# A float32 transformer kernel on one core: the first blocks of the FFN and of the MLPs get an order of their own, and two helpers move behind them

## The reference

```python
# model 1, behind the attention: D_FF = 2816
h = rms_norm(x, norm2_g)
x = x + (silu(h @ w_gate) * (h @ w_up)) @ w_down

# model 2, in each of two layers: MLP_HIDDEN = 4096
u = rmsnorm(x, norm_mlp[l])
x = x + jnp.square(jax.nn.relu(u @ w_mlp_up[l])) @ w_mlp_down[l]

def rmsnorm(x, g):
    return x * lax.rsqrt(jnp.mean(x * x, axis=-1, keepdims=True) + EPS) * g
```

## Time and profile before

| | us |
|---|---|
| median of 3 runs | 1058.37 |
| lowest and highest | 1055.93 and 1059.07 |
| the profiled execution, its device time | 1054.6 |
| its span, from the first to the last instruction | 1052.8 |
| PE busy in the span | 1030.9 (98%) |
| DVE busy | 708.2 (67%) |
| ACT busy | 535.8 (51%) |
| mean granted clock of TensorE | 0.992 |

### The profile page before, as it was taken

One profiled execution on the slowest core, in us unless ns is written; L12 is line 12 of the kernel. 1 busy time (PEld: TensorE's weight loads), 2 busy tenths in 40 slices (PEclk: granted clock), 3 DMA queues, 4 the chain that ended last, 5 costly groups with the idle time before them and its releaser, 6 DMA issues.

```text
span 1052.8 us, 16387 instructions
## 1 busy us (share of the span) xinstructions
PE 1030.9 (98%) x6205; PEld 896.1 (85%) x6205; DVE 708.2 (67%) x1073; ACT 535.8 (51%) x687; POOL 69.7 (7%) x80
## 2 busy tenths in 40 slices
PE   8999999999999999999999999999999999999997
PEld 6865778888888899998788888888999988888886
DVE  6886766666667686768766656667776777655655
ACT  6546565444457535555635444475354646544443
POOL 1000000000000309000000000011270000000000
PEclk8999999999999999999999999999999999999999
DMA  9964326555556653258365563665632665566521
GB/s 293 246 225 145 120 89 232 200 174 195 174 185 195 200 166 121 81 176 297 128 219 181 189 210 106 225 203 166 192 101 80 230 230 180 179 201 199 165 94 40
DMA packets 130652, 185.12 MB, mean 176 GB/s; under 512 B 4361, under 2 KB 106399, under 8 KB 130591
## 3 DMA queue, kind: packets, MB, share of 16 engines
q1 hardware_dynamic: 130503, 184.25, 54.0%
q10 hardware_dynamic: 88, 0.04, 0.0%
HBM read 180.91 MB, written 1.56 MB: 173 GB/s over the span
## 4 chain that ended last, share of the span: by engine, by line
PE 90%; SPq 2%; ACT 2%; DMA 2%; DVE 2%; issue 1%; ACTq 0%; DVEq 0%
PE wide L559 18%; PE wide L566 9%; PE acc L522 9%; PE acc L523 9%; PE acc L524 9%; PE wide L522 7%; PE wide L523 7%; PE wide L524 7%; PE wide L542 3%; PE wide L535 3%; PE wide L536 3%; DMA raw<-in_w_in 1%; PE acc L702 1%; ACT whi L976 1%; SPq L436 1%; PE acc L736 1%
## 5 line engine op out<-in xcount | busy, mean ns | idle before, releaser
L1270 DVE TENSOR_TENSOR wlo<-raw,whi 128x2048 fp32r<-128x2048 f32 (+1 forms) x178 | 386.8, 2180 | 155.6 <-ACT whi L976 154.5
L976 ACT ACTIVATE whi<-raw 128x2048 fp32r<-128x2048 f32 (+1 forms) x178 | 321.9, 1819 | 106.1 <-PE wide L524 43.9
L559 PE MATMUL wide<-uhl,whi 128*128 128x512 f32 x864 | 208.2, 392 | 0.0
L559 PEld LDWEIGHTS wide<-uhl,whi 128*128 128x128 f32 x864 | 160.9, 188 | 33.9 <-DVE uhl L1295 1.2
L522 PE MATMUL acc<-whi,mhi 128*128 128x512 f32 x376 | 147.9, 393 | 3.0 <-DVE wlo L1270 2.7
L522 PE MATMUL wide<-uhl,whi 128*128 128x256 f32 x512 | 147.5, 288 | 0.8 <-DVE wlo L1355 0.8
L523 PE MATMUL acc<-wlo,mhi 128*128 128x512 f32 x376 | 146.8, 390 | 0.0
L524 PE MATMUL acc<-whi,mlo 128*128 128x512 f32 x376 | 146.4, 389 | 0.0
L523 PE MATMUL wide<-uhl,whi 128*128 128x256 f32 x512 | 145.5, 284 | 0.0
L524 PE MATMUL wide<-uhl,wlo 128*128 128x256 f32 x512 | 145.5, 284 | 0.0
L566 PEld LDWEIGHTS wide<-uhl,wlo 128*128 128x128 f32 x864 | 111.7, 193 | 4.4
(11 more groups left out here) (248 smaller groups left out, 1212.1 us busy)
## 6 DMA issues: line engine op xcount, KB each, us to landing
raw<-in_w_in SPq DMA_DIRECT2D x49, 1024.0 KB, 5.3
raw<-in_w_mlp_up SPq DMA_DIRECT2D x32, 1024.0 KB, 5.5
raw<-in_w_mlp_down SPq DMA_DIRECT2D x32, 1024.0 KB, 4.9
raw<-in_w_gate SPq DMA_DIRECT2D x11, 1024.0 KB, 5.4
raw<-in_w_up SPq DMA_DIRECT2D x11, 1024.0 KB, 5.5
raw<-in_w_down SPq DMA_DIRECT2D x11, 1024.0 KB, 5.5
raw<-in_w_mix_out SPq DMA_DIRECT2D x8, 1024.0 KB, 6.6
raw<-in_w_out SPq DMA_DIRECT2D x4, 1024.0 KB, 9.6
```

Source lines behind the costliest of these rows:

```text
L559: pe.matmul(col[2 * n + c][:], whi_v(u)[:, f, c * P:c * P + P], uhl[:, f, :], start=f == 0, stop=False)
L976: act.activation(whi[:, u.buf, 0:size], raw[:, u.slot, 0:size], ACT.Copy).then_inc(w_hi, 1)
L1270: dve.tensor_tensor(wlo[:, u.buf, 0:size], raw[:, u.slot, 0:size], whi[:, u.buf, 0:size].bitcast(F32), ALU.subtract).then_inc(w_lo, 1)
```

## The change

In the FFN, PE's `spread_rn` moves from the middle of the first up unit (unit 15) to behind the whole of it, and its wait for rb_sb moves from ahead of the first loop block to the first down unit. Two new semaphores, ff_a and ff_d, tell PE that the banks of a gate or an up unit have been read; ff_g and ff_ok no longer let PE go on. On ACT and DVE the first blocks (0, 1 and 2) are written out ahead of the loop: the splits of units 17 and 18 come between the parts of block 0, the copy of rnb comes behind both bank reads, and the scaling by rnb behind the sums. The loops run from the second turn on.

In the MLP, the split of the first down unit (L_MLP + 2) moves ahead of the first block's `low_half` on ACT and ahead of its `ff_split` on DVE. The sum of squares on ACT moves behind block(0), and DVE's two small steps on rn behind block(1). The three blocks that were written out behind ACT's and DVE's loop stand ahead of it now.

The diff, cut to its core:

```diff
@@ -315,6 +315,8 @@
+        ff_a = sem("ff_a")
+        ff_d = sem("ff_d")
@@ -840,16 +842,18 @@
             wide_features_after(1, a_unit(A_FF), 0)
-            wide_features(a_unit(A_FF + 1), 1, lambda: spread_rn(acc[3], 2))
-            pe.wait_ge(rb_sb, 2)
+            wide_features(a_unit(A_FF + 1), 1)
+            spread_rn(acc[3], 2)
             def ff_block(q, turns, start):
                 gate, up, down = (a_unit(A_FF + 2 + 3 * q + r, turns) for r in range(3))
-                pe.wait_ge(ff_g, 2 * turns + q + 1)
+                pe.wait_ge(ff_a, 2 * turns + q + 1)
                 wide_features(gate, 0)
-                pe.wait_ge(ff_ok, 2 * turns + q + 1)
+                pe.wait_ge(ff_d, 2 * turns + q + 1)
                 wide_features(up, 1)
+                if start:
+                    pe.wait_ge(rb_sb, 2)
                 pe.wait_ge(w_lo, down.upto())
                 pe.wait_ge(ff_lo, 2 * turns + q + 1)
                 rows(down, mid(mhi, q), mid(mlo, q), start, False)
@@ -1134,17 +1138,19 @@
             split(a_unit(A_FF + 2))
             squares(1)
             deviations(1)
-            spread_rn(acc[3], 2)
-            def ff_gate(q, count, gate):
+            def gate_low(q, gate):
                 act.wait_ge(used, gate.upto())
                 act.activation(ff_e[q].rearrange("p (c t) -> p c t", c=2), wide[0][:, :, T:2 * T], ACT.Copy).then_inc(ff_b, 1)
+            def gate_sigmoid(q, count):
                 act.wait_ge(ff_g, count)
                 act.activation(ff_h[q], ff_e[q], ACT.Sigmoid).then_inc(ff_act, 1)
-            def ff_up(q, up):
+            def up_low(q, up):
                 act.wait_ge(used, up.upto())
                 act.activation(ff_e[1 - q].rearrange("p (c t) -> p c t", c=2), wide[1][:, :, T:2 * T], ACT.Copy).then_inc(ff_c, 1)
@@ -1153,19 +1159,34 @@
                 act.wait_ge(ff_ok, count)
                 act.activation(mid(mhi, s), h.rearrange("p (c t) -> p c t", c=2), ACT.Copy).then_inc(ff_hi, 1)
-            ff_gate(0, 1, a_unit(A_FF))
-            ff_up(0, a_unit(A_FF + 1))
+            def ff_block(q, turns):
+                j, b = A_FF + 2 + 3 * q, (1 + q) % 2
+                gate_low(b, a_unit(j, turns))
+                gate_sigmoid(b, 2 * turns + q + 2)
+                split(a_unit(j + 3, turns))
+                up_low(b, a_unit(j + 1, turns))
+                ff_split(ff_h[b], b, 2 * turns + q + 2)
+            def ff_weights(q, turns):
+                split(a_unit(A_FF + 3 + 3 * q, turns))
+                split(a_unit(A_FF + 4 + 3 * q, turns))
+            gate_low(0, a_unit(A_FF))
+            split(a_unit(A_FF + 3))
+            up_low(0, a_unit(A_FF + 1))
+            spread_rn(acc[3], 2)
+            gate_sigmoid(0, 1)
+            split(a_unit(A_FF + 4))
             ff_split(ff_h[0], 0, 1)
-            with act.Fori(0, LOOPS) as i:
+            ff_block(0, 0)
+            ff_weights(1, 0)
+            ff_block(1, 0)
+            with act.Fori(1, LOOPS) as i:
                 for q in range(2):
-                    j = A_FF + 2 + 3 * q
-                    b = (1 + q) % 2
-                    split(a_unit(j + 1, i))
-                    split(a_unit(j + 2, i))
-                    ff_gate(b, 2 * i + q + 2, a_unit(j, i))
-                    split(a_unit(j + 3, i))
-                    ff_up(b, a_unit(j + 1, i))
-                    ff_split(ff_h[b], b, 2 * i + q + 2)
+                    ff_weights(q, i)
+                    ff_block(q, i)
@@ -1236,22 +1257,25 @@
                     act.activation(mlp_h[s].rearrange("p (c t) -> p c t", c=2), wide[n][:, :, T:2 * T], ACT.Copy).then_inc(ff_act, 1)
                 split(l_unit(l, L_MLP + 1))
-                squares(3 + 2 * l)
+                split(l_unit(l, L_MLP + 2))
                 low_half(0, 0, l_unit(l, L_MLP))
                 ff_split(mlp_h[0], 0, done + 1)
                 def block(q, turns, count):
                     s = (1 + q) % 3
-                    split(l_unit(l, L_MLP + 2 + 2 * (q % 3), turns))
+                    if q:
+                        split(l_unit(l, L_MLP + 2 + 2 * (q % 3), turns))
                     split(l_unit(l, L_MLP + 3 + 2 * (q % 3), turns))
                     low_half(s, (1 + q) % 2, l_unit(l, L_MLP + 1 + 2 * (q % 3), turns))
                     ff_split(mlp_h[s], s, count)
+                block(0, 0, done + 2)
+                squares(3 + 2 * l)
+                block(1, 0, done + 3)
+                block(2, 0, done + 4)
                 with act.Fori(0, 2) as i:
                     for q in range(6):
-                        block(q, 2 * i + q // 3, done + 6 * i + q + 2)
-                for q in range(3):
-                    block(q, 4, done + 12 + q + 2)
+                        block(3 + q, 2 * i + 1 + q // 3, done + 6 * i + q + 5)
@@ -1516,44 +1540,73 @@
             split(a_unit(A_FF + 1))
             split(a_unit(A_FF + 2))
             inverse(2)
-            dve.wait_ge(rb_sb, 2)
-            def scale_gate(q, count):
+            def gate_sum(q, count):
                 e = ff_e[q].rearrange("p (c t) -> p c t", c=2)
                 dve.wait_ge(ff_b, count)
-                link(dve.tensor_tensor(e, wide[0][:, :, 0:T], e, ALU.add))
+                dve.tensor_tensor(e, wide[0][:, :, 0:T], e, ALU.add).then_inc(ff_a, 1)
+            def gate_scale(q, count):
+                e = ff_e[q].rearrange("p (c t) -> p c t", c=2)
+                dve.wait_ge(ff_a, count)
                 dve.tensor_tensor(e, e, rnb[:].unsqueeze(1).broadcast_to([P, 2, T]), ALU.mult).then_inc(ff_g, 1)
-            def swiglu(q, count):
-                e, h = ff_e[q], ff_h[q]
+            def up_sum(q, count):
                 v = ff_e[1 - q].rearrange("p (c t) -> p c t", c=2)
+                dve.wait_ge(ff_c, count)
+                dve.tensor_tensor(v, wide[1][:, :, 0:T], v, ALU.add).then_inc(ff_d, 1)
+                dve.wait_ge(ff_d, count)
+            def swish(q, count):
                 dve.wait_ge(ff_act, count)
-                dve.tensor_tensor(h, h, e, ALU.mult)
-                dve.wait_ge(ff_c, count)
-                link(dve.tensor_tensor(v, wide[1][:, :, 0:T], v, ALU.add))
-                dve.tensor_tensor(h, h, ff_e[1 - q], ALU.mult).then_inc(ff_ok, 1)
+                return dve.tensor_tensor(ff_h[q], ff_h[q], ff_e[q], ALU.mult)
+            def gated_up(q):
+                dve.tensor_tensor(ff_h[q], ff_h[q], ff_e[1 - q], ALU.mult).then_inc(ff_ok, 1)
             def ff_split(h, s, count):
                 dve.wait_ge(ff_hi, count)
                 dve.tensor_tensor(mid(mlo, s), h.rearrange("p (c t) -> p c t", c=2), mid(mhi, s).bitcast(F32),
                                   ALU.subtract).then_inc(ff_lo, 1)
-            scale_gate(0, 1)
-            swiglu(0, 1)
+            def ff_block(q, turns):
+                j, b, count = A_FF + 2 + 3 * q, (1 + q) % 2, 2 * turns + q + 2
+                gate_sum(b, count)
+                gate_scale(b, count)
+                split(a_unit(j + 3, turns))
+                swish(b, count)
+                up_sum(b, count)
+                gated_up(b)
+                ff_split(ff_h[b], b, count)
+            def ff_weights(q, turns):
+                split(a_unit(A_FF + 3 + 3 * q, turns))
+                split(a_unit(A_FF + 4 + 3 * q, turns))
+            gate_sum(0, 1)
+            split(a_unit(A_FF + 3))
+            up_sum(0, 1)
+            dve.wait_ge(rb_sb, 2)
+            gate_scale(0, 1)
+            link(swish(0, 1))
+            gated_up(0)
+            split(a_unit(A_FF + 4))
             ff_split(ff_h[0], 0, 1)
-            with chain.loop(LOOPS, 4) as i:
+            ff_block(0, 0)
+            ff_weights(1, 0)
+            ff_block(1, 0)
+            with chain.loop(LOOPS - 1, 0) as i:
                 for q in range(2):
-                    j = A_FF + 2 + 3 * q
-                    b = (1 + q) % 2
-                    split(a_unit(j + 1, i))
-                    split(a_unit(j + 2, i))
-                    scale_gate(b, 2 * i + q + 2)
-                    split(a_unit(j + 3, i))
-                    swiglu(b, 2 * i + q + 2)
-                    ff_split(ff_h[b], b, 2 * i + q + 2)
+                    ff_weights(q, i + 1)
+                    ff_block(q, i + 1)
@@ -1663,24 +1716,27 @@
                 done = FF_BLOCKS + MLP_BLOCKS * l
                 split(l_unit(l, L_MLP + 1))
+                square(0, 0, done + 1)
+                split(l_unit(l, L_MLP + 2))
+                ff_split(mlp_h[0], 0, done + 1)
+                def block(q, turns, count):
+                    s = (1 + q) % 3
+                    if q:
+                        split(l_unit(l, L_MLP + 2 + 2 * (q % 3), turns))
+                    split(l_unit(l, L_MLP + 3 + 2 * (q % 3), turns))
+                    square(s, (1 + q) % 2, count)
+                    ff_split(mlp_h[s], s, count)
+                block(0, 0, done + 2)
+                block(1, 0, done + 3)
```

(13 more changed lines are left out.)

## The result

| | before | after |
|---|---|---|
| median of 8 runs, us | 1057.55 | 1050.62 |
| lowest and highest | 1052.47 and 1060.66 | 1045.39 and 1053.83 |
| ratio after to before, 95% interval | | 0.9931 (0.9910 to 0.9951) |
| span of the profiled execution | 1052.8 | 1049.0 |
| mean granted clock | 0.992 | 0.993 |

The account below looks back on a forecast made before the run. PE, busy 98% of the span, was taken as the bound. The FFN's 3.99 us and the MLPs' 3.26 us sum to 7.25 us, so 1058.37 - 7.25 = 1051.1 us, range 1047.0 to 1055.5.

Parts of the forecast that it names:

- The FFN's term: FFN start, unit 15 to unit 16: 10.03 us would become 6.04, a gain of 3.99 us.
- the stall and the clock: Two parts of the FFN gain: 2.19 us of PE's stall before the spread and 1.80 us of lower clock behind it.
- The margins in the FFN: Time in hand before PE needs the gate's banks, 1.2 us, the up's banks, 2.7, and the first down unit, 2.0.
- The MLP's term: PE's wait for wlo before each MLP's first down unit goes: 1.63 us per layer, 3.26 us for both.
- The thin margin: MLP, first down unit: DVE's low part would be ready 0.4 us before PE wants it.
- that of the second down unit: MLP: DVE's split of the second down unit would end 1.0 us before PE wants it.
- One of the signs: Each MLP's first down unit would start 11.04 us or so behind the start of its second up unit's block.
- The rival on the clock: FFN: the clock's 1.80 us does not come back, giving 1052.9 us; chance 0.12.
- The rival on the MLP: PE would wait for mlo or the second down unit's wlo instead; 1054.4 us if all 3.26 stay; chance 0.10.
- The rival further on: PE's stalls are made up later, at a transfer or another engine, giving 1057 to 1058 us; chance 0.06.
- slower rival: FFN and MLP loops: each jump back costs a 2.59 us instruction fetch, 12.95 us in all, giving 1064.1 us; chance 0.04.
- shift of 3.8 us: The profile-based time, 1047.4 us, lay 3.8 us below the median of the runs shown; the difference was taken to the median.

Follow-up runs that it names:

- ffn_alone: The change's FFN edits with the MLP code of the kernel before; 1053.68 us, ratio 0.9960 to before.
- before_warm: Kernel before plus 9 matmuls of zeros ahead of the spread; one execution, 912.67 us from unit 15 to the end, against 914.37 before.
- ffn_old_order: Changed kernel with FFN block 0 in the old order on ACT and DVE; one execution, 908.93 us from unit 15 to the end, against 907.15 changed.
- mlp_alone: The change's MLP edits with the FFN code of the kernel before; 1056.31 us, ratio 0.9979 to before.
- squares_early: Changed kernel with the MLP squares back ahead of ACT's first copy; one execution, 909.73 us from unit 15 to the end, against 907.15 changed.
- loops_only: Kernel before with only ACT's and DVE's first blocks written out ahead of the loops, nothing reordered; 1057.63 us, ratio 1.0001 to before.
- spread_only: Kernel before with only PE's spread moved behind the whole first up unit; one execution, 913.05 us from unit 15 to the end, against 914.37 before.
- squares_only: Changed kernel with the split of the MLPs' first down unit put back; one execution, 910.34 us from unit 15 to the end, against 907.15 changed.
- after_warm: Changed kernel plus 10 matmuls of zeros ahead of PE's wait for the convolution input's shifted copies; 1048.78 us, ratio 0.9913 to before.

## Why the prediction was right

- **The FFN's term**, 3.99 us forecast: 4.10 by ffn_alone, 4.2 by its timed runs. Within it the stall and the clock were right; from unit 15 to unit 16 it took 5.93 us, 6.04 were said, as the spread costs 0.36 us from start to start when PE does not stop before it. The 1.80 us that the prediction gave to the clock hold some 0.25 us that PE needs to start again behind the stop; before_warm has 1.55 for the clock alone.
- **The margins in the FFN**, 1.2, 2.7 and 2.0 us in the forecast, are 1.2, 3.0 and 2.4. ffn_old_order shows what the order is for, by a walk through the same rows: 1.5 us expected, 1.58 measured. ACT_TABLE_LOAD ahead of the sigmoid, 1.28 us, was left out of the walk; it lay where ACT had to wait for DVE anyway.
- **The MLP's term**, 3.26 us: 3.27 where the waits were, 2.96 by mlp_alone and 7.22 - 4.10 = 3.12 by the whole. The thin margin was 0.4 us in the forecast and is 0.5; that of the second down unit 1.0 and is 1.2. One of the signs was written down wrongly: the first down unit starts one unit behind the second up unit, 5.56 us (509.69 to 515.25), not 11.04, which is what a block takes.
- **The rival on the clock** (its part does not come back) falls, by the timed runs of ffn_alone, whose interval of 2.9 to 5.5 us excludes the 2.2 us without it. The timed runs of the whole change could not have told it from the forecast, as 7.25 - 1.80 = 5.45 lies within 5.2 to 9.5. In three profiles with the old FFN the clock fell there each time, and before_warm gives the part back, in one execution. The doubt itself was sound: the prediction had one profile, and the wait of 2.03 us for prob, the same in all thirteen, was followed by a fall in eight only.
- **The rival on the MLP** (stalls in another form) falls by the waits after. squares_early shows the form it would have had.
- **The rival further on** (the gain made up elsewhere) falls: the measure reaches to the end of the span and holds the sum but for 0.15 us (4.10 + 3.27 = 7.37 at the places themselves, 7.22 to the end), which is within its scatter. The **slower rival** (fetches) falls by loops_only.
- What the prediction left out is the scatter of the first 140 us. It took the profiled execution's time to the median by a shift of 3.8 us without asking where that came from. The profile of before had the shortest wait for the transfers of the first ten (1.9 us) and the clock at 1.00 behind the wait for prob; the profile after had neither. Whoever had compared the two spans would have found half the gain. And that the medians differ by 6.9 us, 0.3 from the forecast, is in part luck, as their interval is 4 us wide; the close check is the 7.22 us of the traces.

## What to carry to other kernels

When PE is the bound, write down for each of its waits the time at which the thing is ready and at which PE could use it, and walk the new order through with measured durations; the margins came out within 0.4 us of that. Edits of this kind come in groups: with one member of a group left out, PE stood still for 1.0 to 2.5 us at the same place or one unit further on (spread_only, ffn_old_order, squares_early, squares_only). Look, too, whether the clock fell behind a stall in one profile only: at the wait for prob this alone was 1.65 us. And compare two profiles from a point behind what scatters, not by their spans: here one gave 7.22 us and the other 3.8.

## What the runs showed of the hardware that was not expected

- The granted clock fell behind PE's stall of 2.15 to 2.19 us before the spread in each of three profiles (0.83 over the ten us from unit 15 on in each), and stayed at 1.00 behind one of 2.53 us in spread_only and of 2.4 us at 54 us in ffn_alone. The wait of 2.03 us for prob was followed by a fall in eight of thirteen profiles and by none in five. The length of a stall alone doesn't tell it, and neither does its place in the kernel. A fall cost 1.55 us before the spread (by before_warm) and 1.65 us behind the wait for prob.
- With matmuls of zeros in the gap the clock was 1.00 behind it in the one profile each of before_warm and after_warm. In before_warm they cost nothing: the matmuls behind the spread started 4.66 us behind unit 15, as without them.
- PE's wait for the sixteen small transfers was 1.9 to 6.2 us in ten profiles of kernels that are the same up to there. SP took 12.2 to 14.0 us to issue them in these ten. What holds the last of them back in one execution and not in another stays open.
